# Scan slot of a hybrid SSD / attention layer: outputs behind the first projection pieces, mix last on VectorE, and the last four pieces spread over four slots

## What is computed

```python
proj = h @ w_in                       # z, xbc, dt, q, k, v, g_a, g_b
scores = einsum('bclhn,bcshn->bclsh', Ch, Bh)
y_diag = einsum('bclsh,bcshp->bclhp', scores * decay_in, xdt)
chunk_states = einsum('bclhn,bclh,bclhp->bchpn', Bh, decay_to_end, xdt)
state, prev = scan(chunk_decay, chunk_states)          # over the chunks
y_off = einsum('bclhn,bchpn,bclh->bclhp', Ch, prev, exp(a_cs))
y = y_f + flip(y_b) + d_skip * xs
y = rmsnorm(y * silu(z), ssd_norm_w)
merged = sigmoid(g_a) * (y @ w_ssd_out) + sigmoid(g_b) * y_attention
```

## Time and profile before

| what | value |
|---|---|
| median of 3 runs | 2761.56 us (2760.55 to 2767.19) |
| profiled execution, its own time | 2762.55 us |
| its span | 2760.8 us |
| mean granted clock of TensorE | 0.958 |
| busy, share of the span | PE 91%, PEld 80%, DVE 77%, ACT 41%, POOL 31% |
| the scan phase | about 626 to 1087 us of the span |

### The profile page before, as it was taken

One profiled execution on the slowest core, in us unless ns is written; L12 is line 12 of the kernel. 1 busy time (PEld: TensorE's weight loads), 2 busy tenths in 40 slices (PEclk: granted clock), 3 DMA queues, 4 the chain that ended last, 5 costly groups with the idle time before them and its releaser, 6 DMA issues. The chain is left out here.

```text
span 2760.8 us, 39138 instructions
## 1 busy us (share of the span) xinstructions
PE 2520.0 (91%) x14998; PEld 2205.5 (80%) x14998; DVE 2125.2 (77%) x3681; ACT 1139.0 (41%) x1946; POOL 866.1 (31%) x623
## 2 busy tenths in 40 slices
PE   5989999988999996988799887999999999999996
PEld 4868888787778775988788586888888888888885
DVE  3657777713788875433699795999999999999998
ACT  4235556524565654322443385232333323333332
POOL 0000000003667663110044284344334433434431
PEclk9999999998999997999899998999999999999998
DMA  6531122223224222533222268999999999999995
GB/s 242 220 113 51 66 100 83 81 95 119 98 77 134 88 68 84 180 109 112 95 78 64 94 201 313 417 419 409 417 416 416 418 413 414 418 414 417 416 406 231
DMA packets 166266, 621.50 MB, mean 225 GB/s; under 512 B 14880, under 2 KB 83264, under 8 KB 105664
## 3 DMA queue, kind: packets, MB, share of 16 engines
q1 hardware_dynamic: 124608, 340.03, 33.2%
q0 software_dynamic: 36864, 268.45, 23.6%
q10 hardware_dynamic: 4608, 10.52, 1.2%
HBM read 559.39 MB, written 59.56 MB: 224 GB/s over the span
## 5 line engine op out<-in xcount | busy, mean ns | idle before, releaser
L2324 POOL DMA_INDIRECT p_uv<-in_uv_rows,merged x256 | 396.3, 1548 | 624.8 <-DVE merged L2491 564.1
L2491 DVE SCALAR_TENSOR_TENSOR merged<-p_uv,p_sw,merged 128x1024 f32<-128x1024 f32 x256 | 330.7, 1292 | 7.1
L2474 DVE CUSTOM_DVE_ANT_0 p_uv<-p_uv,merged 128x1024 f32<-128x1024 f32 x256 | 310.2, 1228 | 17.5 <-DMA p_uv<-in_uv_rows,merged 17.5
L2344 PE MATMUL p_pa<-h2D,w_hi 128*128 128x384 f32 x896 | 318.8, 356 | 4.5 <-DVE w_lo L2445 2.3
L2346 PE MATMUL p_pa<-h2D,w_lo 128*128 128x384 f32 x896 | 302.7, 338 | 0.0
L2345 PE MATMUL p_pa<-h2D,w_hi 128*128 128x384 f32 x896 | 302.6, 338 | 0.0
L2388 ACT ACTIVATE w_hi<-w_raw 128x2048 fp32r<-128x2048 f32 x110 | 210.4, 1913 | 177.6 <-DMA w_raw<-in_w_stream 104.9
L2359 PE MATMUL p_py<-w_hi,p_wh 128*128 128x512 f32 x672 | 266.9, 397 | 14.2 <-DVE w_lo L2445 14.0
L2445 DVE TENSOR_TENSOR w_lo<-w_raw,w_hi 128x2048 fp32r<-128x2048 f32 x110 | 251.7, 2288 | 23.7 <-ACT w_hi L2388 23.7
L2361 PE MATMUL p_py<-w_hi,p_wl 128*128 128x512 f32 x672 | 266.0, 396 | 0.0
L2360 PE MATMUL p_py<-w_lo,p_wh 128*128 128x512 f32 x672 | 265.9, 396 | 0.0
(11 more groups left out here) (386 smaller groups left out, 6202.8 us busy)
## 6 DMA issues: line engine op xcount, KB each, us to landing
w_raw<-in_w_stream SPq DMA_DIRECT2D x174, 1024.0 KB
g_pairs<-e_st SPq DMA_DIRECT2D x5, 4096.0 KB, 16.4
p_g<-g_pairs SPq DMA_DIRECT2D x64, 320.0 KB
t_ada<-in_w_ada SPq DMA_DIRECT2D x16, 1024.0 KB, 10.2
xc_dram<-c_xc SPq DMA_DIRECT2D x8, 1284.0 KB, 5.4
p_ve<-in_v_early SPq DMA_DIRECT2D x8, 1024.0 KB, 13.9
r_ur<-in_u_early ACTq DMA_DIRECT2D x14, 512.0 KB, 3.7
s_xx<-xc_dram SPq DMA_DIRECT2D x8, 642.0 KB, 6.3
```

Of the source, the lines that this page charges most:

```text
L2324: nc.gpsimd.indirect_dma_start(uv[:, k % RING, :], None, K.uv_rows, bass.IndirectOffsetOnAxis(K.sidx[:, t, c:c + 1], 0)).then_inc(K.gather ...
L2344: nc.tensor.matmul(ps_a[m][:, :], wh[:, k, cols], K.h2D[0][:, k, :], start=k == 0, stop=False)
L2474: nc.vector.tensor_tensor_reduce(uv[:, b, 0:D], uv[:, b, 0:D], K.hrow[:, t, :], 1.0, 0.0, ALU.mult, ALU.add, sa[:, at:at + 1]).then_inc(do ...
L2491: nc.vector.scalar_tensor_tensor(ys[:, t, :], uv[:, b, D:2 * D], sw[:, at:at + 1], ys[:, t, :], ALU.mult, ALU.add).then_inc(v_done, 1)
```

## The change

No instruction is added or removed. Three things are moved: on PE `outputs(f)` goes from the start of the slot to behind the first pieces; on DVE `masks` goes ahead of `finish`, and `mix` behind `weighted`; the table of pieces gives 68 pieces to slots 0 to 39 and one each to the next four that the formula reaches.

```diff
@@ phase_ssd
     def pieces_by(q):
-        return 0 if q < 0 else min(len(PIECES), (q + 1) * len(PIECES) // (STEPS + 2))
+        last = len(PIECES) - 4
+        if q < 0:
+            return 0
+        return (q + 1) * last // STEPS if q < STEPS else last + min(4, q - STEPS)
@@ tensor
                 a, b, f = ssd_steps(q)
                 todo = pieces_of(q)
-                if f is not None:
-                    outputs(f)
                 if 1 <= q <= STEPS:
                     states(q - 1)
                 if b is not None:
                     between(b)
                 for u, i in todo[:split_point(todo)]:
                     piece(u, i)
+                if f is not None:
+                    outputs(f)
                 if a is not None:
                     transposes(a)
@@ vector
                 a, b, f = ssd_steps(q)
+                if b is not None:
+                    masks(b)
                 if f is not None:
                     finish(f)
-                if b is not None:
-                    masks(b)
-                    mix(b)
                 if a is not None:
                     weighted(a)
+                if b is not None:
+                    mix(b)
                 for u in last_pieces(q - 1):
                     S.lo(dve, U_ZG + u + 2, u % 2)
```

## The result

The changed kernel takes 2769.71 us (median of 20 runs), the kernel before 2759.95 (20 runs beside them): a ratio of 1.0035 with a 95% interval of 1.0026 to 1.0043, **9.8 us slower**. The direction is the forecast one, the size is half of the 18.6 us forecast. The profiled execution took 2769.28 us (span 2767.6, clock 0.956), so it stands for the median.

A forecast was written before the change was run, and what follows sets the result against it. TensorE was taken to bound the scan body. Body losses of 66 us against 43.7 (+22.3) and -3.7 for the tail with slot 40's order gave +18.6 on 2762.55; with the median 1.0 lower, 2780.0 us, range 2752 to 2794.

The forecast's parts named there:

- What bounds the scan: Scan body: TensorE bounds it; its waits for `s_M` fall from 26.9 to under 10 us, for `s_xs` rise from 8.4 to 35 or more.
- The ten one-piece slots: Scan body: `s_xs` waits of 3.35 us in six slots with full `finish` (20.1), 1.9 in four with short `finish` (7.6).
- the double carry: Scan body, three short slots: chunk 0's double carry costs 2.4 us in all.
- the clock as a whole: Scan body: TensorE's slow clock after holes, ten one-piece slots at 1.4 us and some long ones: 16, bounds 0 and 28.
- z second pieces: Scan body, 12 two-piece slots whose second piece is z: 0.4 us lost in each, 4.8 in all.
- Collisions behind a weight split: Scan body, 12 slots: the split starts GpSimd's chain 2.3 us late, so it runs into `finish` and `weighted`; 12.3 us.
- The bare time: Slots 6 to 39: pieces 179.6 us plus small products 134.2, 313.8 us without losses; 43.7 were lost before the change.
- The tail: From slot 40's y products to the scan's end: 44 us against 50.8, -6.8; slot 42 takes 12.9 for GpSimd's rT.
- part 2: Order inside slot 40: y products stand behind states and between (2.1 us), plus 1.0 for the products themselves; +3.1 us.
- faster: Rival, scan body: 3.3 us holes leave the clock alone and GpSimd's late chain never meets `finish`; 2752, chance 0.17.
- No change: Rival: the clock alone is spared (-16), +2.6, or the tail's gains are a little larger; 2764, chance 0.13.
- Worse: Rival, scan body: GpSimd meets `finish` in every slot, 1.1 us more in 22 further slots; 2796 to 2804, chance 0.10.

The follow-up runs named there:

- the filler: Changed kernel with 20 unneeded matmuls (12 where `finish` is short) ahead of the state product after each one-piece slot; 2753.57 us, ratio 0.9973.

## Why the prediction was right in direction and half in size

1. *What bounds the scan* held. The M wait went (26.9 to 1.4, forecast under 10), the xs wait came (8.4 to 37.5, forecast 35 or more), in holes of 1.9 to 4.2 us right behind the transposes of the one-piece slots, L1425 at 0.69, the clock at 0.94. That both halves of the order make this wait is shown by runs: `weighted` first takes back 10 us, transposes first as well 13.
2. *The ten one-piece slots* were priced at 3.35 and 1.9 us for the wait, 27.7 in all, plus 6.0 for collisions, 2.4 for the double carry and 14 for the clock: 50.1. They lose 51.2, but that it fits is partly luck. The holes were forecast at 36.1 (27.7 + 6.0 + 2.4) and measure 30.7; the clock was forecast at 14, and 20.4 us are lost beyond the holes, 18.4 of them to the clock by the filler. Two errors of about 5 us cancel. In the same way the clock as a whole, 16, meets the 15.8 of the filler only because the other 24 slots lose 2.7 us more there.
3. **The step that failed is the sum over the 24 two-piece slots: 15.9 us forecast, 6.2 measured.** (The prediction gives 12.3 for all collisions behind a weight split; 6.0 and 6.3 are my division of it. By its own 1.6 for a short slot, the six one-piece slots behind a split, 10, 20, 23, 26, 33 and 36, would hold 9.6, and the two-piece slots would be forecast at 12.3: still twice the 6.2, and still most of the miss. Splits stand ahead of 13 slots, not 12.) Its four terms: z second pieces 4.8, about 3.6 came (0.3 instead of 0.4 each). Collisions behind a weight split 6.3, about 3.1 came: the slots 12, 15, 28 and 39 lose 0.74, 0.83, 1.22 and 1.21 us (three of them with the 0.3 in it), slots 7, 17 and 31 nothing of it. ScalarE's silu and table loads in slots 19 and 35 at 2.8, nothing came: the copy is later, but `weighted` stands behind `finish` anyway. The clock in long slots at 2, nothing: their holes are 1.0 us at most. The bare time is some 0.06 us a slot too long, which makes up the rest. I had added up delays of three engines in slots where a second piece of 2.8 or 3.5 us stands ahead of the wait as cover.
4. *Weight split and GpSimd.* Moving the split gave back 9.4 us of body loss, where I had 12.3, but 7.5 of it beyond the holes of the one-piece slots, most of which is the clock, which I had booked apart; the holes themselves shrank by 3.1. The row's price, 0.79 for 0.42, was no bound: `finish` instructions of the changed kernel reach 0.95 us (L1442 at 783.32). The Trainium skill, "SBUF — State Buffer", section "Who interferes with whom", has the engine that issues first keep the shared pair of ports for its whole instruction while the other blocks. The trace agrees to the hundredth of a us: an add or product of 128x256 with two inputs in SBUF that starts while an instruction of GpSimd runs takes its own 0.42, plus what is left of GpSimd's instruction, less 0.14. In slot 23 that is 0.63, 0.72 and 0.82 for the measured 0.63, 0.72 and 0.83, and it holds within 0.01 us for all 41 instructions of this size on VectorE with two inputs from SBUF that took over 0.5 us in the changed kernel. So what the prediction worked out from the page, a whole instruction of GpSimd for each operation, was the worst case of the rule and not its usual price: VectorE waits only for the rest of it.
5. *The tail* came to 43.0 us from the end of slot 40's y group (forecast 44) and part 2 to 2.6 (forecast 3.1), but not by my mechanism. I had 12.9 us up to slot 42's y group for GpSimd's `s_rT`; it took 6.4 from slot 41's. Instead slot 40's y group to slot 41's took 12.95 where I had 7.5, for **ScalarE's** half of `s_rT`. I had followed GpSimd's chain and never ScalarE's, which has the z unit's end in slot 39. The total was right by chance.
6. Sum: the body came 8.6 us under its forecast (13.7 for 22.3), most of it step 3 (9.7, less 1.1 more in step 2), the tail 1.5 under (-5.2 for -3.7). The forecast of slot 40's y group at 1060 stands against 1051.15 for the first reason. The scan's +8.5 reached the program as +6.7 in this execution and as +9.8 in the medians; the difference lies within the spread of the runs (2762.66 to 2774.17).

Of the rivals, "faster" fell with the filler. "No change" had the clock spared, which the filler refutes as well, though its number, 2764, lay nearer to the result than mine. "Worse", GpSimd meeting `finish` in every slot, did not happen: L1449 has a median of 0.425.

## What to carry to other kernels

In a software pipeline, an order that frees an engine is worth nothing by itself: here 77 us of VectorE's busy time went and the kernel became slower, since one short product was put behind work that waits for TensorE. Put first on each engine what the bounding engine needs next, and follow that through *every* engine on the chain (transposes, ScalarE's copy, product), since moving it up on one only exposes the next: 10, 13, then 21 us. Price a hole in TensorE with the slow clock behind it, here three fifths as much again as the holes themselves (18.4 for 30.7 us), and price delays against their cover, slot by slot, not as a sum. A product that is moved up may land beside GpSimd: `weighted`, moved ahead of `finish`, took 16.6 us for 10.7 in the ten slots that matter.

## What the hardware did that was not expected

- Ten holes of 1.9 to 4.2 us in a TensorE stream that was otherwise full cost 18.4 us of clock, 1.4 to 2.8 each. In the kernel with the early split, holes of 1.50 us and one of 2.79 (slot 16) cost none, nor did holes of 2.15 and 2.58 (slots 16 and 23) in the kernel with `weighted` first alone, so the length of the hole alone does not decide; what does is open. Matmuls that compute nothing of use, placed in the holes, gave the clock back: 0.94 to 1.00 over 360 us. They took no time of their own, since TensorE was waiting: the ten holes sum to 30.5 us with them and to 30.7 without.
- Moving one elementwise instruction of 2.28 us (the weight split) by a few places on VectorE was worth 9 us in the changed kernel, though VectorE is idle a quarter of the time. It sets when GpSimd starts, and so which instructions meet; the larger part of the gain was the clock of TensorE behind somewhat shorter holes.
- VectorE and GpSimd slow each other to 1.41 and 1.55 us for instructions that take 0.69 and 1.04 apart, and the same 3681 instructions of VectorE take 77 us less in the changed order, though the program is longer. The busy share of 77% before was no measure of how near VectorE was to being the bound.
- A short instruction of VectorE that is caught by one of GpSimd waits for the rest of it: 0.42 became 0.95 in the changed kernel, and 1.30 with `token_major` ahead, where 1.02 us of a 1.04 us instruction were left.
